# One MoE decoder step: an idle buffer takes expert 3's down matrix, the scattered rows are fetched later, and VectorE adds by tiles

## The reference

```python
h2 = rms_norm(x, norm_ffn).reshape(b * s, D_MODEL)
x = x + moe_ffn(h2, ...)          # 4 groups x 8 SwiGLU experts, top 1 group, top 2 experts
gate = sigmoid(rms_norm(x, norm_ple) @ w_ple_gate)
x = x + gate * (pemb @ w_ple_proj)
y = rms_norm(x, final_norm)
...
y_e = (silu(xb @ w_gate[e]) * (xb @ w_up[e])) @ w_down[e]   # per expert, then times the row's weight
```

## Time and profile before

| what | value |
|---|---|
| median of 3 runs | 1079.02 us (1077.35 to 1079.91) |
| the profiled execution's own time | 1078.77 us |
| its span, first to last instruction | 1077.0 us |
| TensorE busy | 1045.3 us, 97% of the span |
| VectorE, ScalarE busy | 285.9 and 239.2 us |
| mean granted TensorE clock | 0.993 of full speed |

### The profile page before, as it was taken

One profiled execution on the slowest core, in us unless ns is written; L12 is line 12 of the kernel. 1 busy time (PEld: TensorE's weight loads), 2 busy tenths in 40 slices (PEclk: granted clock), 3 DMA queues, 4 the chain that ended last, 5 costly groups with the idle time before them and its releaser, 6 DMA issues.

```text
span 1077.0 us, 14385 instructions
## 1 busy us (share of the span) xinstructions
PE 1045.3 (97%) x5798; PEld 538.6 (50%) x5798; DVE 285.9 (27%) x767; ACT 239.2 (22%) x492; POOL 91.2 (8%) x133
## 2 busy tenths in 40 slices
PE   8999999999999999999999999999999999999894
PEld 4478887555666667775543333333333333333342
DVE  1132011566334314121441111111111111122342
ACT  2021001266322243000141411111111111111153
POOL 0020040000222220000000000000000000001000
PEclk9999999999999999999999999999999999999997
DMA  9980248220645578553288999999999999999920
GB/s 331 277 280 5 78 99 176 78 79 1 167 151 161 177 287 198 226 212 140 79 334 334 424 427 427 425 429 427 428 428 427 428 428 425 427 428 424 333 93 30
DMA packets 58215, 288.93 MB, mean 268 GB/s; under 512 B 10195, under 2 KB 14524, under 8 KB 45550
## 3 DMA queue, kind: packets, MB, share of 16 engines
q1 hardware_dynamic: 48270, 259.61, 62.2%
q0 software_dynamic: 9648, 28.43, 9.2%
q10 hardware_dynamic: 240, 0.09, 0.0%
HBM read 277.87 MB, written 19.55 MB: 276 GB/s over the span
## 4 chain that ended last, share of the span: by engine, by line
PE 52%; DMA 10%; issue 1%; DVE 0%; ACT 0%; POOL 0%; SPq 0%; POOLq 0%
PE ps L1173 17%; PE ps L587 9%; PE ps L1201 8%; DMA late<-in_w_exp_up_dram 7%; PE ps L1145 4%; DMA reg_o<-in_w_exp_down_dram 3%; PE ps L1070 3%; PE ps L658 2%; PE ps L1158 1%; PE ps L1149 1%; PE ps L606 1%; PE ps L1189 1%; PE ps L1041 1%; PE ps L665 1%; PE ps L629 1%
## 5 line engine op out<-in xcount | busy, mean ns | idle before, releaser
L1173 PE MATMUL ps<-ring,reg_xh 128*64 128x512 f32 x512 | 148.7, 595 | 4.3 <-DMA ring<-in_w_exp_up_dram 2.7
L1173 PE MATMUL ps<-late,reg_xh 128*64 128x512 f32 x336 | 148.6, 595 | 1.2 <-DMA reg_k<-in_w_exp_up_dram 1.2
L1173 PEld LDWEIGHTS ps<-ring,reg_xh 128*64 128x64 f32 x512 | 46.7, 137 | 88.0 <-issue 85.3
L2173 DVE TENSOR_TENSOR reg_xh<-reg_xh,ps 64x512 f32<-64x512 f32 x32 | 22.1, 691 | 232.6 <-ACT reg_xh L1571 232.6
L1571 ACT ACTIVATE reg_xh<-ps 64x512 f32<-64x512 f32 x32 | 34.0, 1064 | 217.3 <-PE ps L1173 217.3
L1173 PE MATMUL ps<-reg_k,reg_xh 128*64 128x512 f32 x176 | 77.8, 595 | 0.0
L2392 POOL DMA_INDIRECT y_rows<-reg_xh,slot_row x29 | 28.3, 975 | 546.6 <-ACT reg_xh L1582 505.5
L883 PE MATMUL ps<-reg_xh,ring 128*128 128x320 f32 x256 | 73.5, 436 | 0.0
L1173 PEld LDWEIGHTS ps<-late,reg_xh 128*64 128x64 f32 x336 | 44.4, 137 | 45.7 <-issue 45.2
L587 PE MATMUL ps<-reg_xh,ring 128*128 128x320 f32 x224 | 60.9, 433 | 0.0
L1145 PE MATMUL ps<-reg_xh 128*64 128x512 f32 x256 | 60.6, 592 | 0.0
(11 more groups left out here) (410 smaller groups left out, 1340.4 us busy)
## 6 DMA issues: line engine op xcount, KB each, us to landing
ring<-in_w_exp_gate_dram SPq DMA_DIRECT2D x21, 2048.0 KB, 21.5
ring<-in_w_in_dram SPq DMA_DIRECT2D x12, 2048.0 KB, 11.4
ring<-in_w_exp_down_dram SPq DMA_DIRECT2D x11, 2048.0 KB, 25.0
ring<-in_w_exp_up_dram SPq DMA_DIRECT2D x11, 2048.0 KB, 26.0
late<-in_w_exp_gate_dram SPq DMA_DIRECT2D x10, 2048.0 KB, 22.0
reg_k<-in_w_exp_up_dram SPq DMA_DIRECT2D x10, 2048.0 KB, 26.7
late<-in_w_exp_up_dram SPq DMA_DIRECT2D x10, 2048.0 KB, 25.7
reg_xh<-in_w_exp_down_dram SPq DMA_DIRECT2D x10, 2048.0 KB, 25.7
```

The costliest lines, as they stand in the source:

```text
L1173: last = pe.matmul(out[64 * part:64 * part + 64, :], xb[:, k, :], ws_[part][:, k, :], start=(k == 0), stop=(k == KT - 1))
L2173: dve.tensor_tensor(sg.rearrange("p (m q) -> p m q", m=4), sg.rearrange("p (m q) -> p m q", m=4), ps[64:128, 2 + par, :].rearrange("p (q m ...
```

## The change

Four things change. (1) `DOWN_SLOTS` gives the down matrices other slots: expert e % 3 = 0 uses slot 7, e % 3 = 1 slot 0, e % 3 = 2 slot 8. Expert 3's down matrix is loaded in two halves ahead of the loop: the first straight behind the stores of `pp_rows`, the second behind `pp_out`, with no wait for a down product. The first turn of the loop is written out (`load_next(4, 1)`, expert 4's down into slot 0, `load_next(5, 2)`, `load_next(6, 0)`, `load_down(5, 2)`), and TensorE waits for the new slots and counts. (2) The second half of `w_ple_gate` goes to slot 7 in place of slot 0. (3) GpSimd waits for `combined` >= 1 before it fetches the rows back. (4) VectorE does tile 0 to its end before the rows of tile 1.

```diff
@@ -43,6 +43,7 @@
 NEG = -1e30
 TILES = ((0, 128), (128, 128), (256, 64))
 EXPERT_SLOTS = ((5, 6, 0), (1, 2, 7), (3, 4, 8))
+DOWN_SLOTS = (7, 0, 8)
 STORED = NE - 3
 COPIES = 16
 
@@ -299,7 +300,7 @@
         gath = [[slots[3 + k][:, 1024 * t:1024 * t + 1024] for t in range(3)] for k in range(2)]
         w_proj = [reg_o[:, 1024 * k:1024 * k + 1024] for k in range(2)]
         pp_rows_sb = [reg_o[:, 2048 + 1024 * t:3072 + 1024 * t] for t in range(2)] + [reg_x[:, 6144:6656]]
-        w_pg = [slots[a].rearrange("p (k n) -> p k n", k=8) for a in (5, 0)]
+        w_pg = [slots[a].rearrange("p (k n) -> p k n", k=8) for a in (5, 7)]
         gain_f = slots[1][:, 0:1024]
         ysb = slots[1][:, 1024:4096].rearrange("p (t n) -> p t n", t=3)
         pgate = reg_x[:, 3072:6144].rearrange("p (t n) -> p t n", t=3)
@@ -516,16 +517,29 @@
             def load_down(e, p):
 
                 sp.wait_ge(down_done, e - 2)
-                load_weights(e, 2, EXPERT_SLOTS[p][2])
-
-            for part, (done, sems) in enumerate(((half_done, [early_in] * 2), (up_done, [chunk_in[slot] for slot in EXPERT_SLOTS[0][0:2]]))):
+                load_weights(e, 2, DOWN_SLOTS[p])
+
+            def load_part(part, done, sems):
+
                 sp.wait_ge(done, 1)
                 for j in range(2):
                     src = exp_src[j][0, 3].rearrange("(p m) n -> p (m n)", p=128)
                     cols_ = slice(2048 * part, 2048 * part + 2048)
                     sp.dma_start(slots[EXPERT_SLOTS[0][j]][:, cols_], src[:, cols_]).then_inc(sems[j], 16)
+
+            down_3 = w_exp_down[0, 3].rearrange("(p m) n -> p (m n)", p=128)
+            sp.dma_start(slots[7][:, 0:2048], down_3[:, 0:2048]).then_inc(early_in, 16)
+            load_part(0, half_done, [early_in] * 2)
             sp.wait_ge(pp_out, 48)
-            with sp.Fori(1, 10) as i:
+            sp.dma_start(slots[7][:, 2048:4096], down_3[:, 2048:4096]).then_inc(chunk_in[7], 16)
+            load_part(1, up_done, [chunk_in[slot] for slot in EXPERT_SLOTS[0][0:2]])
+            load_next(4, 1)
+            sp.wait_ge(down_done, 1)
+            load_weights(4, 2, DOWN_SLOTS[1])
+            load_next(5, 2)
+            load_next(6, 0)
+            load_down(5, 2)
+            with sp.Fori(2, 10) as i:
                 for p in range(3):
                     load_next(i * 3 + p + 1, (p + 1) % 3)
                     load_down(i * 3 + p, p)
@@ -555,7 +569,7 @@
                     sp.wait_ge(ov["down"], e * EXTRA + 1)
                     for j in range(3):
                         src = exp_src[j][0, bass.ds(e, 1)].rearrange("a (p m) n -> p (a m n)", p=128)
-                        sp.dma_start(slots[(1, 2, 7)[j]], src).then_inc(ov["chunks"], 16)
+                        sp.dma_start(slots[(1, 2, 0)[j]], src).then_inc(ov["chunks"], 16)
                 sp.wait_ge(ov["down"], NE * EXTRA + 1)
 
 
@@ -1243,10 +1257,10 @@
                     gate_up(slots[w_gate], slots[w_up], xe[par], ps[:, 2 + par, :], half_done).then_inc(up_done, 1)
                 else:
                     if keep == -2:
-                        pe.wait_ge(early_in, 80)
+                        pe.wait_ge(early_in, 96)
                     gate_up(slots[w_gate], slots[w_up], xe[par], ps[:, 2 + par, :]).then_inc(up_done, 1)
                 if not first:
-                    w_down = before_spare_down() if keep == -3 else before_down(i, p)
+                    w_down = {-4: before_first_down, -3: before_spare_down}[keep]() if keep in (-4, -3) else before_down(i, p)
                 if not last_one:
                     gather(sel[1 - par], ps[:, 1 - par, :], sel_ready, e + 2, gathered)
                 if first:
@@ -1269,21 +1283,28 @@
                 e, turn_no = i * 6 + p - 1, i * 2 + (p - 1) // 3 + 1
                 pe.wait_ge(he_ready, e + 1)
                 pe.wait_ge(ye_ready, e + 1)
-                slot = EXPERT_SLOTS[(p - 1) % 3][2]
-                if (p - 1) % 3 == 1:
+                slot = DOWN_SLOTS[(p - 1) % 3]
+                if slot == 7:
                     turn_no = turn_no - 1
                 pe.wait_ge(chunk_in[slot], (turn_no + uses[slot]) * 16)
                 return rows_of(slot)
 
+            def before_first_down():
+
+                pe.wait_ge(he_ready, 1)
+                pe.wait_ge(ye_ready, 1)
+                pe.wait_ge(chunk_in[0], (1 + uses[0]) * 16)
+                return rows_of(0)
+
             def before_spare_down():
 
                 pe.wait_ge(he_ready, 2)
                 pe.wait_ge(ye_ready, 2)
-                pe.wait_ge(early_in, 80)
+                pe.wait_ge(early_in, 96)
                 return spare
 
             for p in range(6):
-                expert(0, p, {0: -1, 2: -3, 3: -2}.get(p))
+                expert(0, p, {0: -1, 1: -4, 2: -3, 3: -2}.get(p))
             with pe.Fori(1, 4) as i:
                 for p in range(6):
                     expert(i, p)
@@ -1331,7 +1352,7 @@
                         pe.wait_ge(ov["sg"], n)
                         turn(ps[:, 6, :]).then_inc(ov["turned"], 1)
                         pe.wait_ge(ov["he"], n)
-                        down(rows_of(7), he[0], ps[:, 5, :]).then_inc(ov["down"], 1)
+                        down(rows_of(0), he[0], ps[:, 5, :]).then_inc(ov["down"], 1)
                 pe.wait_ge(ov["ye"], NE * EXTRA + 1)
                 last_stage()
 
@@ -2237,9 +2258,9 @@
             most = dve.value_load(route[:, :].bitcast(I32)[0:1, 1019:1020], min_val=0, max_val=N)
             with dve.If(most <= SLOTS):
                 main_rows(0)
-                main_rows(1)
                 add_sums(0)
                 copy_x2(0)
+                main_rows(1)
                 add_sums(1)
                 main_rows(2)
                 add_sample_sums()
@@ -2394,6 +2415,7 @@
             pool.wait_ge(ye_out[0], (STORED // 2 + 1) * 16)
             pool.wait_ge(ye_out[1], STORED // 2 * 16)
             pool.wait_ge(up_done, NE - 2)
+            pool.wait_ge(combined, 1)
             for t, (t0, rows) in enumerate(TILES):
                 for k in range(2):
                     pool.dma_start(gath[k][t][0:rows, :], y_rows[N * k + t0:N * k + t0 + rows, :]).then_inc(rows_back[t], 16)
```

## The result

The changed kernel takes 1082.28 us, the median of 18 runs (1080.68 to 1084.56), against 1077.6 us for the kernel before in 18 runs beside them (1075.14 to 1081.76). The ratio is 1.0043 with a 95% interval of 1.0034 to 1.0053. It is slower by 0.4%; the prediction had said 0.24% faster, with 0.13 on slower, and the time lies above its range. The profiled execution took 1080.84 us, its span is 1079.2 us and its mean granted clock 0.988.

What follows compares the result with a forecast made beforehand. The expert loop was taken to begin bound by TensorE and end bound by DMA. `gated` starting 2.6 us earlier took 1078.77 to 1076.2, so 1076.4 us for the median; forecast range 1075.0 to 1077.0, 8 in 10 within 1074.0 to 1079.5.

Steps and rivals of the forecast that it cites:

- The lead: In the expert loop: loading expert 3's down matrix early gains 2.0 us, lasting to the end; the later fetch adds 0.6.
- Parts 2 and 4 at nothing: The other slot for `w_ple_gate` costs nothing, and VectorE's order moves no work; its chain fits with 0.7 us to spare.
- R: Arrival of tile 0's fetched rows before its turning, taken as 1016.5 us; no loss to 1014.5, no gain left at 1019.1.
- the bounds (1013.5 and 1026.8): Limits for R: below from a GpSimd store with idle queues (2.9 us), above from the earlier second fetch (17.4 us).
- the 1.5 us "for start and landing": Allowance for the fetch's start and landing, added to 8.1 us of transfer when estimating R as 1018.4.
- The estimate by the rate of the earlier trace: Fetch of tile 0's rows at GpSimd's earlier rate, 0.52 MB in 4 us: 8.1 us plus 1.5, so R = 1018.4.
- the prediction's 4.8 us: From R to the end of tile 0's turning: two adds, two sums, the last four transposes and handing over.
- rival (a): Tile 0's rows come late: R = 1026.8, time 1086.7 us; decides above R = 1019.1; chance 0.17.
- Rival (b): Behind a fair fetch, tile 1 or 2's rows or TensorE's clock (1.5 us lost) stall: about 1077.9 us; chance 0.18.
- The forecast's own case: Start of `gated` 2.6 us earlier with R = 1016.5: 1075.0 to 1077.0 us around 1076.4; chance 0.48.
- 1078.77: Time in us of the profiled execution before the change, from which the forecast took 2.6 us, giving 1076.2.

## Why the prediction was wrong

**The lead: right.** Forecast 2.0 us from the idle buffer and 0.6 from the moved fetch. The early load alone made the loop 1.9 us shorter and the kernel 2.8 us faster by the ratio (1.2 to 4.3), the late fetch alone made the loop 0.6 us shorter, both together 2.7 to 3.1. The idle time came back before 604 us, expert 6's gate landed in 8.2 us (8.1 taken), and the two waits for down matrices went. The waits for up matrices repeat best: 5.0 to 5.2 us in the three traces with the loop and fetch of before, 2.2 to 2.5 in six of the eight with the changed ones.

**Parts 2 and 4 at nothing: right**, by the early load alone and by the order alone.

**R, the arrival of tile 0's rows: the step that failed first.** The prediction put the fetch at 1008.8 and R at 1016.5, 7.7 us later. The first copy was issued at 1007.69 and R was 1018.35, 10.66 us later. Counted from expert 31's start, R was to come 1016.5 - 994.8 = 21.7 us behind it and came 1018.35 - 993.41 = 24.9 behind it: 3.2 us late. It lies inside the bounds (1013.5 and 1026.8).

The term that was mis-sized is the 1.5 us "for start and landing". The first packet alone started 3.9 us after the issue, and what followed took 6.8 us where 7.7 - 1.5 leaves 6.2. So 2.4 us of the miss are the start and 0.6 the transfer. The estimate by the rate of the earlier trace rows, 8.1 + 1.5 = 9.6 us, came nearer to 10.66 by luck: its transfer was too long and its start too short.

The late start could have been read beforehand. In the trace of before, the fetch was issued at 990.45 and its first packet started at 994.22, 3.8 us later. Over the fourteen traces it is 3.7 to 3.9 us in the ten in which SP's last issue lies 0.7 to 2.1 us ahead of the fetch, and 1.3 to 1.5 us in the four in which it lies over 15 us ahead (the fetch at expert 31's product, or SP held back, each with and without the late load of `final_norm`). Busy engines alone do not make it: with the fetch at expert 31's product their share was 0.83 in the 1.3 us before the first packet. Holding SP back takes the late start away; by what mechanism SP's loads cause it was not tested.

The second half of the gate matrix did run out on the way, as the prediction said: 976 of its 1024 packets had started before the first packet of the rows, though the last ones straggled and it landed only at 1022.97. What the prediction left out is what SP issues behind it, the three loads of `pp_rows` at 1004.71, 1006.34 and 1006.91. They now stand ahead of the fetch; before the change they stood behind it. From 1011.59 to 1017.1 us they moved 0.91 MB beside 1.07 MB of rows. No run holds back the half matrix and the `pp_rows` loads apart, so what each costs stays open.

The Trainium skill ("DMA: Bandwidth & Descriptors", Queues, rings and completion order) says that an engine takes turns among its queues. The trace agrees once the rows have started: 262 packets of them and 223 of `pp_rows`, all of 4096 bytes, moved in those 5.5 us, although `pp_rows` was issued first. Taking turns does not save the fetch: it only gets its share.

**The clock: the second step, and it was priced as a rival of its own.** By itself this R is no disaster. The run began 1.3 us early, so on the clock of the earlier trace rows R is 1019.7, the turning ends at 1024.5 by the prediction's 4.8 us, and that is 0.6 us behind the old 1023.92: rival (a) just past its point, 1079.4, within 0.2%. What makes it slower is that the wait it causes is 5.36 us long. Rival (b) had the clock, with 1.5 us and for waits of 1.4 us. It fell not behind those (the trace of before had them at full clock) but inside the long one, and cost 0.88 us on the transposes and 2.25 on the product, 3.1 in all; filling the wait gave 2.7 back. 1078.77 + 0.6 + 3.1 = 1082.5, less the early 1.3 us 1081.2, and the profiled execution took 1080.84. That 1082.5 also lies near the median, 1082.28, is luck: the 1078.77 it starts from is 1.2 us above what eighteen runs of the kernel before gave, 1077.6. The Trainium skill ("TensorE: Matmul & The Clock Gate", Part 1) has the slow clock as the default, which activity lifts; by the earlier trace rows alone I had held that against it, but those rows showed only short waits.

**The error in the chances.** (a) and (b) were treated as alternatives, 0.17 and 0.18, when the first brings the second: a late R is a long wait, and a long wait costs the clock. The forecast's own case held a wait of 1 to 2 us before the turning, and every us by which R is later adds one. The point from which (a) is slower by 0.2% was set at R = 1021.3 without the clock; with its 3.1 us the point is near 1018.2, if the clock also falls in the shorter wait of that case. No run tried that before the transposes; the nearest is the wait of 2.45 us before L672, which cost 1.5 us of clock. The rate of the earlier trace rows had given R = 1018.4, right at that point. Joined, the two rivals should have had far more than 0.13 on slower.

**What remains.** Prediction and median are 5.9 us apart, 4.6 in the profiled execution. The forecast was worked from a median of three runs, 1079.02, and eighteen gave 1077.6; side by side, the change costs 4.7 us where 2.6 were to be won. Measured in the tail the miss is 3.2 (R) + 0.7 (the rest of the way to L643, mostly the slower transposes) + 2.25 = 6.2 us; against it stands the earlier start of 1.3 us. 0.3 us is left in the profiled execution, below what runs scatter.

Two slips changed nothing. The rates of 424 to 429 GB/s stand in slices 22 to 36, not 37, counted from 0. And rival (a)'s 1086.7 adds its 7.7 us to 1079.0, the median, while the sum goes from 1078.77, which gives 1086.5.

## What to carry to other kernels

When a transfer is moved later, list what every other queue will have issued by then: freeing a queue also lets its next loads go, and they delay the start of the transfer that is now urgent and share the engines with it. Read the start of a transfer, from its issue to its first packet, from the trace at hand instead of assuming it (here 1.3 or 3.9 us). Price a wait of TensorE together with the clock behind it (here 3 us after 5 us of waiting, 1.5 after 2.45), not "late" and "slow clock" as separate cases. If the order of need is known, let the less urgent queue wait for the urgent landing; here one such line turned 0.4% slower into 0.3% faster.

## What the hardware showed that was not expected

- TensorE's clock: waits of 1.4 us left it at 1.00; waits of 5.36, 5.88 and 6.31 us were each followed by 0.50 that began inside the wait. One of 2.45 us was followed by a shorter spell at 0.50, which began inside the wait too (L672 at 8.62 us instead of 7.11), one of 0.85 us by none. Matmuls on constants in the gap kept it at 1.00.
- GpSimd's first packet started 3.7 to 3.9 us after the issue where SP had issued 0.7 to 2.1 us before, and 1.3 to 1.5 us after it where SP had not for 15 us. The reason was not found.
- The same 512 KB copy, second in GpSimd's queue, took 4.6 us with few other packets, 8.3 to 11.0 beside SP's loads of 2 KB and 4 KB packets, and 17.4 beside 16 KB packets.
- At a DMA share of 1.0 the engines moved 428 GB/s in the expert loop, 405 from 1010 to 1014 us in the changed kernel, and 252 from 1010 to 1014 in the kernel before. Packets of 4096 bytes took 165 ns in the fast stretches and, averaged over 2 us, 240 to 440 in the slow ones. Neither the one-row read of `final_norm` nor tile 2's copies is the whole cause; what is was not found.
